# x and projection weights loaded in pieces over 128 partitions, in a hybrid decoder block

## What is computed

```
h = rms_norm(x, ln_g)                         # x * rsqrt(mean(x*x) + eps) * ln_g
proj = h @ w_in                               # 1024 -> 2816 columns
(u_pool, g_pool, c_a, c_b, g_conv, q, k, v, g_attn) = split_columns(proj)
y_pool = pool_mixer(u_pool, pool_w, pool_scale)
y_conv = conv_module(c_a, c_b, ...)           # 31 taps
y_attn = sliding_window_attention(q, k, v, attn_sinks)   # window 128, 8 heads, 2 key heads
y = concat(y_pool * silu(g_pool), y_conv * silu(g_conv), y_attn * silu(g_attn))
out = rms_norm(x + y @ w_out, final_g)
```

## Time and profile before

| | |
|---|---|
| median of three runs | 1468.76 us |
| the profiled execution | 1470.4 us, its span 1468.7 us |
| TensorE matmul busy | 1409.4 us, 96% |
| TensorE weight load busy | 1149.3 us, 78% |
| VectorE busy | 1192.1 us, 81% |
| ScalarE busy | 552.6 us, 38% |
| GpSimd busy | 380.7 us, 26% |
| DMA | 196.90 MB, mean 134 GB/s |
| granted TensorE clock | 0.984 of full speed |

### The profile page before, as it was taken

One profiled execution on the slowest core, in us unless ns is written; L12 is line 12 of the kernel. 1 busy time (PEld: TensorE's weight loads), 2 busy tenths in 40 slices (PEclk: granted clock), 3 DMA queues, 4 the chain that ended last, 5 costly groups with the idle time before them and its releaser, 6 DMA issues.

```text
span 1468.7 us, 20096 instructions
## 1 busy us (share of the span) xinstructions
PE 1409.4 (96%) x6814; PEld 1149.3 (78%) x6814; DVE 1192.1 (81%) x2453; ACT 552.6 (38%) x1428; POOL 380.7 (26%) x592
## 2 busy tenths in 40 slices
PE   6897999999898989999999999999999999999998
PEld 4775878687777868787788888888888888888886
DVE  5585868777686857575999999889899998888886
ACT  5463555564554545441221122112222243333332
POOL 5122231322332232311010110100101245555552
PEclk9998999999999999999999999999999999999999
DMA  9517163544517070636330330321326756455531
GB/s 204 169 54 215 47 186 107 143 150 101 185 57 219 10 228 15 164 152 129 129 129 15 144 129 15 129 105 52 129 83 243 284 171 216 163 163 158 160 134 72
DMA packets 90389, 196.90 MB, mean 134 GB/s; under 512 B 14928, under 2 KB 56272, under 8 KB 82640
## 3 DMA queue, kind: packets, MB, share of 16 engines
q1 hardware_dynamic: 75760, 181.40, 38.1%
q10 hardware_dynamic: 14560, 14.68, 3.7%
HBM read 114.27 MB, written 81.79 MB: 133 GB/s over the span
## 4 chain that ended last, share of the span: by engine, by line
PE 74%; DVE 12%; DMA 8%; SPq 3%; ACT 2%; issue 1%; DVEq 0%; POOLq 0%; POOL 0%; ACTq 0%
PE wide L337 12%; PE wide L335 12%; PE wide L336 12%; PE pair L1116 7%; PE pair L1117 7%; PE pair L1120 7%; DMA xs<-in_x_dram 6%; DVE m_tail L1867 3%; DVE xT L328 2%; PE wide L1134 2%; PE wide L1135 2%; PE pair L1098 2%; PE pair L337 2%; PE turn L337 2%; PE turn L336 2%; PE pair L336 2%
## 5 line engine op out<-in xcount | busy, mean ns | idle before, releaser
L1867 DVE SCALAR_TENSOR_TENSOR m_tail<-m_tail,m_taps 128x512 f32<-128x512 f32 x480 | 338.6, 754 | 4.6
L1116 PE MATMUL pair<-xT,w_hi 128*128 128x512 f32 x632 | 258.4, 409 | 12.1 <-DVE y_out L991 5.6
L1120 PE MATMUL pair<-xT,w_hi 128*128 128x512 f32 x632 | 252.7, 400 | 0.0
L1117 PE MATMUL pair<-xT,w_lo 128*128 128x512 f32 x632 | 252.6, 400 | 0.0
L107 POOL TENSOR_TENSOR pool_carrier<-pool_carrier 128x1 f32<-128x1 f32 x77 | 27.0, 350 | 680.8 <-DVE m_meanvar L1876 402.8
L1116 PEld LDWEIGHTS pair<-xT,w_hi 128*128 128x128 f32 x632 | 122.8, 194 | 41.0 <-DVE y_out L991 6.0
L1120 PEld LDWEIGHTS pair<-xT,w_hi 128*128 128x128 f32 x632 | 121.9, 193 | 31.1 <-DVE xT L328 2.8
L1620 POOL TENSOR_TENSOR operand_sums<-m_y 128x512 f32<-128x512 f32 x75 | 102.0, 1360 | 167.8 <-PE wide L337 116.6
L1117 PEld LDWEIGHTS pair<-xT,w_lo 128*128 128x128 f32 x632 | 122.4, 194 | 22.9
L759 POOL TENSOR_SCALAR a_rows<-a_rows,a_inv 128x128 f32<-128x128 f32 x256 | 108.0, 440 | 76.5 <-DVE a_inv L945 76.5
L335 PE MATMUL wide<-x_first,w_hi 128*128 128x512 f32 x320 | 125.5, 392 | 0.0
(11 more groups left out here) (259 smaller groups left out, 2957.2 us busy)
## 6 DMA issues: line engine op xcount, KB each, us to landing
xT_scratch<-xT SPq DMA_DIRECT2D x16, 2048.0 KB, 7.7
xs<-in_x_dram SPq DMA_DIRECT2D x32, 512.0 KB, 10.7
x_first<-xT_scratch SPq DMA_DIRECT2D x16, 1024.0 KB, 8.4
xT<-xT_scratch SPq DMA_DIRECT2D x16, 1024.0 KB, 9.3
combo_scratch<-stage SPq DMA_DIRECT2D x28, 512.0 KB, 3.1
m_y<-y_scratch ACTq DMA_DIRECT2D x14, 1024.0 KB, 6.6
y_scratch<-y_out SPq DMA_DIRECT2D x8, 1024.0 KB, 5.8
y_scratch<-y_out SPq DMA_DIRECT2D x16, 512.0 KB, 2.9
```

The costliest lines, as they stand in the source:

```text
L1116: nc.tensor.matmul(out, w_hi, st.hi[:, kk, :], start=(kk == 0), stop=False)
L1117: nc.tensor.matmul(out, w_lo, st.hi[:, kk, :], start=False, stop=False)
L1120: last = nc.tensor.matmul(out, w_hi, st.lo[:, kk, :], start=False, stop=(kk == KT - 1))
L1867: nc.vector.scalar_tensor_tensor(out=conv[:, i, :], in0=h[:, i, j:j + TB], scalar=taps[:, i, j:j + 1], in1=conv[:, i, :], op0=ALU.mult, op ...
```

## The change

The loads of x for blocks 1 to 7 become 16 DMAs, one for each group of 32 tokens; each writes 128 partitions x 1 KB, and its source is read as [4 column blocks][32 tokens][256 columns]. Four of them count on each of the four semaphores, so a semaphore now tells of a quarter of the groups, and `square` and `square_more` wait for one quarter at a time. A chunk of weights becomes 8 DMAs, each 128 partitions x 1 KB with a source of [4][32][256]. The gain comes as 32 runs of 32 values, 4 DMAs of 8 partitions x 128 bytes, into a cleared 128x32 tile, and one 32x32 transpose on VectorE turns it. On SyncE the gain stands ahead of chunk K; x of block 1 is asked for right after chunk G, ahead of G+1 and of the first store of xT, and waits for the scaled rows of block 0 instead of its transposes. The sinks have a semaphore of their own.

```diff
@@ XStage.load, load_gain
         if n == 1:
-            sp.wait_ge(self.turned, KT)
+            sp.wait_ge(self.prepared, self.GAIN_READY + SUB)
         else:
             sp.wait_ge(self.lo_done, KT * n)
-        width = D // SUB
+        for a in range(self.GROUPS):
+            first = n * TB + a * self.SQUARE
+            sp.dma_start(self.groups[:, a], self.x[0, first:first + self.SQUARE].rearrange("s (b c) -> b s c", b=SUB)
+                         ).then_inc(self.loaded[a // SUB], 16)
+
+    def wait_loaded(self, engine, n, part):
+
+        engine.wait_ge(self.loaded[part], 16 + 16 * SUB * n)
+
+    def load_gain(self, sp):
+        sp.wait_ge(self.prepared, 1)
         for b in range(SUB):
-            sp.dma_start(self.groups[b * self.SQUARE:(b + 1) * self.SQUARE],
-                         self.x[0, n * TB:(n + 1) * TB, b * width:(b + 1) * width].rearrange("(a s) c -> s a c", s=self.SQUARE)
-                         ).then_inc(self.loaded[b], 16)
...
+            sp.dma_start(self.gain[b * self.SQUARE:b * self.SQUARE + KT],
+                         self.ln_g[0, b * KT * self.SQUARE:(b + 1) * KT * self.SQUARE].rearrange("(k r) -> k r", k=KT)
+                         ).then_inc(self.prepared, 16)
+
+    def clear_gain(self, dve):
+
+        self.nc.vector.memset(self.gain[:], 0.0).then_inc(self.prepared, 1)
+
+    def turn_gain(self, dve):
+
+        dve.wait_ge(self.prepared, 1 + 16 * SUB)
+        self.nc.vector.transpose(self.gain[:], self.gain[:]).then_inc(self.prepared, 1)
@@ square (square_more alike, with parts 2 and 3)
-        self.wait_loaded(act, n)
         for i in range(self.HALF):
+            if i % SUB == 0:
+                self.wait_loaded(act, n, i // SUB)
@@ Weights.load
         matrix, first, _ = self.plan[c]
-        rows, width = P // SUB, D // SUB
-        for b in range(SUB):
-            sp.dma_start(self.landing[c][b * rows:(b + 1) * rows],
-                         matrix[0, b * width:(b + 1) * width, first:first + CHUNK].rearrange("(k r) c -> r k c", k=KT)
-                         ).then_inc(self.loaded[c], 16)
+        rows = matrix[0, :, first:first + CHUNK].rearrange("(b k r) c -> k b r c", b=SUB, k=KT)
+        for k in range(KT):
+            sp.dma_start(self.landing[c][:, k], rows[k]).then_inc(self.loaded[c], 16)
@@ sync
         st.load(sp, 0)
+        st.load_gain(sp)
         w.load(sp, CHUNK_K)
-        st.load_gain(sp)
-        sp.dma_start(sinks[:], attn_sinks[0:1, :].to_broadcast([P, HEADS])).then_inc(st.vectors_loaded, 16)
-        for c in range(CHUNK_Q, CHUNK_CB):
-            if c == CHUNK_G + 1:
-                sp.wait_ge(w.lo_done[CHUNK_K], 2)
+        sp.dma_start(sinks[:], attn_sinks[0:1, :].to_broadcast([P, HEADS])).then_inc(sinks_loaded, 16)
+        for c in range(CHUNK_Q, CHUNK_G + 1):
             w.load(sp, c)
@@ body(n) of sync
-            store_xT(n, 0)
-            st.load(sp, n + 1)
+            if n == 0:
+                st.load(sp, 1)
+                sp.wait_ge(w.lo_done[CHUNK_K], 2)
+                w.load(sp, CHUNK_G + 1)
+                store_xT(0, 0)
+            else:
+                store_xT(n, 0)
+                st.load(sp, n + 1)
```

More of the change, by code:

```diff
@@ L138 @@
     AHEAD = 5
+    GAIN_READY = 2 + 16 * SUB
     def __init__(self, nc, ctx, x, ln_g, xT, xT_stored, xs, sb):
@@ L150, in __init__ @@
         self.rstd = sb("rstd", [P, self.GROUPS])
-        self.gain = sb("gain", [P, KT])
+        self.gain = sb("gain", [P, self.SQUARE])
         self.fold = sb("fold", [P, P])
@@ L155, in __init__ @@
         self.loaded = [sem(f"x_loaded{s}") for s in range(SUB)]
-        self.vectors_loaded = sem("vectors_loaded")
+        self.prepared = sem("gain_and_first_rows")
         self.squared = sem("x_squared")
@@ L159, in __init__ @@
         self.rstd_steps = sem("rstd_steps")
-        self.scaled = sem("x_scaled")
         self.turned = sem("x_turned")
@@ L181, in load @@
         if n == 1:
-            sp.wait_ge(self.turned, KT)
+            sp.wait_ge(self.prepared, self.GAIN_READY + SUB)
         else:
             sp.wait_ge(self.lo_done, KT * n)
-        width = D // SUB
-        for b in range(SUB):
-            sp.dma_start(self.groups[b * self.SQUARE:(b + 1) * self.SQUARE],
-                         self.x[0, n * TB:(n + 1) * TB, b * width:(b + 1) * width].rearrange("(a s) c -> s a c", s=self.SQUARE)
-                         ).then_inc(self.loaded[b], 16)
-    def wait_loaded(self, engine, n):
-        for b in range(SUB):
[L194 to L201, removed]
+        for a in range(self.GROUPS):
[6 more added lines that the diff above has]
+        sp.wait_ge(self.prepared, 1)
+        for b in range(SUB):
+            sp.dma_start(self.gain[b * self.SQUARE:b * self.SQUARE + KT],
[6 more added lines that the diff above has]
+        self.nc.vector.transpose(self.gain[:], self.gain[:]).then_inc(self.prepared, 1)
     def make_fold(self, pool):
@@ L232, in square_more @@
         width = D // SUB
-        self.wait_loaded(dve, n)
         for i in range(self.HALF):
+            if i % SUB == 0:
+                self.wait_loaded(dve, n, 2 + i // SUB)
             a, out = self.HALF + i, self.more_squares[:, i % SUB * width:(i % SUB + 1) * width]
@@ L257, in first_scale @@
             rows = self.xs[:, s].rearrange("p (b k r) -> p k b r", b=SUB, k=KT)
-            self.nc.vector.tensor_scalar(out, rows, self.rstd[:, s:s + 1], None, ALU.mult).then_inc(self.scaled, 1)
+            self.nc.vector.tensor_scalar(out, rows, self.rstd[:, s:s + 1], None, ALU.mult).then_inc(self.prepared, 1)
     def fold_sums(self, pe, n):
@@ L295, in first_transposes @@
         for s in range(SUB):
-            pe.wait_ge(self.scaled, s + 1)
+            pe.wait_ge(self.prepared, self.GAIN_READY + s + 1)
             for k in range(TURNS):
@@ L315, in split_hi @@
         if n == 0 and k == 0:
-            act.wait_ge(self.vectors_loaded, 16 * SUB + 16)
+            act.wait_ge(self.prepared, self.GAIN_READY)
         if k % PIECE == 0:
@@ L392, in split_hi @@
     def split_hi(self, act, c, half=None):
-        act.wait_ge(self.loaded[c], 16 * SUB)
+        act.wait_ge(self.loaded[c], 16 * KT)
         self.nc.scalar.activation(self.piece(self.hi(c), c, half), self.piece(self.landing[c], c, half),
@@ L606, in attention_programs @@
     constants_made = sem("constants_made")
+    sinks_loaded = sem("sinks_loaded")
     bias_step = sem("bias_step")
@@ L675, in body @@
         def body(n):
-            store_xT(n, 0)
-            st.load(sp, n + 1)
+            if n == 0:
[6 more added lines that the diff above has]
+                st.load(sp, n + 1)
             if n == 1:
                 combos.load_raw(sp, 0, [(0, 1), (1, 1), (0, 0), (1, 0)])
-            st.wait_loaded(sp, n + 1)
+            for part in range(SUB):
+                st.wait_loaded(sp, n + 1, part)
             store_xT(n, 1)
@@ L904, in vector @@
         carrier = dve_carrier
+        st.clear_gain(dve)
         carrier.prepare(dve)
@@ L908, in vector @@
         nc.vector.memset(v[:, 0, :], 0.0).then_inc(constants_made, 1)
+        st.turn_gain(dve)
         st.first_scale(dve)
         w.split_lo(dve, CHUNK_K, 0)
-        dve.wait_ge(st.vectors_loaded, 16 * SUB + 16)
+        dve.wait_ge(sinks_loaded, 16)
         def take_scores(n, j, kv):
@@ L2140, in turn_u @@
         def turn_u():
-            pe.wait_ge(w.loaded[CHUNK_U], 16 * SUB)
+            pe.wait_ge(w.loaded[CHUNK_U], 16 * KT)
             pe.wait_ge(pT_done, ATTENDED)
```

## The result

| | before | after |
|---|---|---|
| median | 1471.7 us (four runs beside those of after) | 1592.7 us (four runs, 1590.3 to 1595.8) |
| span of the profiled execution | 1468.7 us | 1594.1 us |
| TensorE matmul busy | 1409.4 us | 1423.1 us |
| TensorE idle between matmuls | 52.4 us | 164.0 us |
| granted clock | 0.984 | 0.945 |

A forecast was written before the change was run, and what follows sets the result against it. The prediction took TensorE's matmuls, 96% busy, to bound the kernel, with its few waits in the attention stage; 33.0 + 12.7 + 61.0 + 1 = 107.7 us more gave a median of 1576 us, range 1530 to 1650.

The forecast's parts named there:

- block 0: First attention block: G+1 lands late behind other loads, delaying ScalarE by 31.6 us, plus 1.4 us of slow clock: +33.0.
- block 1: Second attention block: x takes 23.6 us instead of 10.9, with the raw w_out pieces still behind it: +12.7.
- blocks 2 to 6: Attention: x +12.7 us per block, quarters give back 1.9, low clock adds 1.4; 12.2 five times: +61.0.
- last block, mixer, output: After block 6: chunks take 7 us more each but mostly have room before use; 0 to 6, taken as +1 us.
- Engines per DMA: New x and weight loads: outermost DRAM count of four puts each DMA on the same four engines; chance 0.79.
- 46 ns for 1 KB: Assumed time of one 1 KB packet on one engine, with 38 and 60 ns as ends; a chunk then takes 11.8 us.
- delay at the copy of v: Block 0: ScalarE was to reach the copy of v at 94.7 instead of 63.08, +31.6 us.
- six matmuls: Block 0: about six matmuls were to run at the lower clock after the long idle time, costing 1.4 us.
- each chunk's 7 us: Last block and mixer: CB, CA, GP, U and GC each take 7 us more, with several to some 20 us of room.
- rival of sixteen engines: New DMAs spread over all sixteen engines, so x lands sooner and fold waits vanish in blocks 2 to 6: 1437 us; chance 0.14.

The follow-up runs named there:

- e1: Changed kernel with each new DMA's outermost count 128 on both sides (values land elsewhere, so only times count): span 1441.8 us.
- e2: Changed kernel with each new DMA's outermost count 8 on the DRAM side (values land elsewhere, so only times count): span 1463.5 us.
- e4: Kernel before with only the weight chunks in the new form; x, gain and order as before: span 1520.6 us (+51.9).
- e3: Kernel before with only x in the new form (16 DMAs, waits by quarter); weights, gain and order as before: span 1546.5 us (+77.8).
- e8: Changed kernel with the four small pool-weight loads ahead of chunk GC on SyncE's queue instead of behind it: span 1580.4 us (-13.7).
- e6: Changed kernel with x and weights in small 32-partition DMAs, x in quarters, chunks in halves, column blocks ordered 0, 2, 1, 3: median 1445.2 us, ratio 0.981 to before.
- e11: e6 with GpSimd's multiplication of y by its gate moved behind the root of the next block's norm: median 1424.1 us, ratio 0.967 to before.
- e5: Changed kernel with x and weight loads back in the old form, leaving only the new gain and SyncE order: median 1463.0 us, ratio 0.994 to before.
- e7: e5 with half of each x load issued on ScalarE's queue: median 1458.5 us, ratio 0.991 to before.
- e9: e6 with the column blocks in the order 0, 1, 2, 3: median 1445.6 us, ratio 0.982 to before.

## Why the prediction was right, step by step

The forecast was 1576 (1530 to 1650), the measured median is 1592.7; on spans 1576.4 against 1594.1. The mechanism was the one forecast (four engines for each new DMA, and the waits that follow from it), and one small term had it wrong. The table takes each block's growth from the fold times (56.89, 135.05, 215.15 before, 81.98, 186.16, 278.26 after, and on) and, in block 0, from where TensorE arrives at its next large wait (122.35 and 160.18).

| step | predicted | measured |
|---|---|---|
| block 0 | +33.0 | +37.8 |
| block 1 | +12.7 | +13.3 |
| blocks 2 to 6 | +61.0 | +57.2 |
| last block, mixer, output | +1 | +17.1 |
| sum | +107.7 | +125.4 |

**Engines per DMA.** Four: right, shown by e1 and e2. That each DMA takes the same four is argued: the share stays at 0.27 while one DMA waits behind the other on the queue, and DMAs on different fours could have run side by side. A share of 0.25 and 85 GB/s were forecast, 0.27 and 89 measured. The 46 ns for 1 KB held: 4 engines x 1024 bytes / 89 GB/s = 46 ns. The forecast's sum went by these 46 ns; its 85 GB/s did not, since 46 ns give 89.

**Block 0.** G+1 was to be split at 91.6 and the copy of v to start at 94.7; they are at 92.10 and 95.26. The mis-sized term is what follows from it. ScalarE, VectorE and TensorE in after:

```profile
92.10 1.91 ACT L401 ACTIVATE w_hi<-a_rows 128x2048 fp32r<-128x2048 f32 x1 [21.86 <-DMA a_rows<-in_w_in_dram]
...
94.04 2.29 DVE L406 TENSOR_TENSOR w_lo<-a_rows,w_hi 128x2048 fp32r<-128x2048 f32 x1 [12.21 <-ACT w_hi L401]
...
97.90 0.55 PE L1149 MATMUL wide<-a_k_hi,a_q 128*128 128x256 f32 x1 [9.05 <-DVE a_q L989]
```

I took the delay at the copy of v (31.6 us), which before had 3.26 us of waiting for TensorE ahead of it, as slack that the delay eats first. The path to TensorE doesn't go through that copy but through VectorE's low parts of G+1 and of q, which had no such slack. The scores' first matmul was at 62.83 and is at 97.90, +35.1; in before:

```profile
62.83 0.28 PE L1134 MATMUL wide<-a_k_hi,a_q 128*128 128x256 f32 x1
```

The other 2.7 us of the 37.8 are clock: 98 to 104 ran at 0.51 where I had put six matmuls, 1.4 us. So 31.6 should have been 35.1 and 1.4 should have been 2.7.

**Block 1.** As forecast: the wait for y_out went from 5.58 to 18.87, the 4.19 of the squares behind it stayed.

**Blocks 2 to 6.** The fold waits grew from 17.6 to 69.3 us, 10.3 for each block, where 12.7 - 1.9 = 10.8 was forecast. The clock was sized right (5.5 us for the five against 7) on a wrong reason: I said that waits of 3 to 4 us did not lower it. They did, as a window of before shows behind the fold wait of 3.75 us in block 3:

```profile
294.50:298.50 4.00, 4.00 (x13) 3.25 (x14) 2.85 (x5) 1.14 (x2) 3.05 (x2) 0.65 0.72 287
```

The page's row of the clock has one digit for each 37 us, and here that is a 9: it hides such stretches. In after the stretch behind such a fold stands at 0.50 (278 to 282), so the low clock is there in both kernels.

**Last block and mixer.** This term failed: +1 against +17.1, nearly all of the difference between forecast and result. I priced each chunk's 7 us against the room before that chunk's own use, and took the later stages to wait for no transfer that the change touches. What was late wasn't a chunk but what stands behind the chunks on SyncE's queue. Behind U and GC are the pool's small loads, and TensorE had 2.6 us of waiting for them before already, so there was no room at all: +12.2. Behind CB, CA and GP is a store of y, for which VectorE waits before it copies the next y; TensorE's wait that follows grew by 2.1 (0.7 to 2.8 in all):

```profile
742.77 21.46 DMA y_scratch<-y_out
```

```profile
764.32 0.69 DVE L1006 COPY y_out<-pair 128x512 f32<-128x512 f32 x1 [4.71 <-DMA y_scratch<-y_out]
...
769.63 2.83 PE L1113 MATMUL pair<-a_pT,a_v 128*64 128x256 f32 x12 [2.33 <-DVE a_pT L968]
```

The remaining 2.8 us are matmuls at a lower clock. The weights make all of this: behind the fold of block 6, e4 is 17.1 us longer than before too, and e3 isn't longer at all. e8 removes the first part. The step asks what is queued behind a slower issue, and I didn't ask it of this queue.

**The rival of sixteen engines** was to give 1437, and e1, which is that case, has 1441.8. The size is close by luck: two errors largely cancel. I said that the fold waits of blocks 2 to 6 would vanish and block 1's get shorter; they don't (1.6 and four of 2.9, and 5.35), since VectorE's squares are slowed by GpSimd (in e1's block 4, too, four of them take 1.5 us, from 351.67 on). That is some 14 us of idle time too much in the forecast gain. What I left out is the clock behind the waits, 11 us less matmul time than before (1398.2 against 1409.4), where I had counted 1.4.

## What to carry to other kernels

Read the pattern of a DMA from both sides before cutting it up: 128 partitions in SBUF are worth nothing if the outermost count on the DRAM side is four. Once the engines per DMA are known, price the transfer at that rate and walk the queue that issues it to its end, small loads behind it included. And where a wait stays although its transfer now lands early, compare one instruction's duration inside and outside the stretch: VectorE's square of 0.42 us that takes 1.5 named a contention whose removal (e6 to e11) was worth 21 us, where the faster loading (e5 to e6) was worth 18.

## What the runs showed of the hardware

- **The clock makes short waits dear.** Waits of 3.2 to 3.8 us always brought some microseconds near the lower level (granted clock 0.54 to 0.76 over 7 us, twelve of twelve), waits of 2.9 us in half the cases. A fold wait shorter by 0.4 us in each of four blocks (e7 to e9) came with 10.8 us less matmul time. The stretches behind the folds make up all of the 10.8 (14.6 against 3.8). Why the same wait of 2.91 us has different consequences from block to block stays open.
- **32-partition DMAs run faster when neighbours write different halves.** In the order 0, 1, 2, 3 they run at 193 GB/s as four large ones and at 212 as sixteen small ones (e9); in the order 0, 2, 1, 3 the small ones run at 231 (e6), and the large ones with one half on each of two queues at 318 (e7). No run puts two queues on the same half, so how much of the 318 is due to the second queue isn't shown. In none of these runs was this rate what the time hung on.
- **GpSimd and VectorE hinder each other by whole instructions**: 0.42 becomes 1.5 us for a square, 0.69 becomes 1.40 for an addition of two SBUF tiles, each time beside a GpSimd multiplication of 1.4 us. It was in the kernel before too. In block 1, where VectorE's squares come late, GpSimd multiplies from 128.07 to 133.57, and the four squares from 128.13 on take 1.5 us; the last three, from 133.79 on, take 0.41:

```profile
128.13 1.51 DVE L237 CUSTOM_DVE_ANT_0 a_pT<-xs 128x256 f32<-128x256 f32 x1
```

So the 4.19 us of waiting for the squares of block 1, which the prediction kept as given, are mostly this.
